# Three 256-column matmuls per weight tile in place of one of 512 and one of 256

## The reference

```
layer 0: x = LN(a*x + even_mixer(x));  x = LN(a*x + conv_ffn(x))     # HGRN2 scan, gated MLP
layer 1: x = LN(a*x + odd_mixer(x));   x = LN(a*x + conv_ffn(x))     # attention with rope
block 2: RG-LRU and dilated attention from one input projection, gates, output projections, RMS norm

conv_ffn(x):  h = x @ w_up                       # 2048 -> 2*5632
              h = conv over 3 tokens + bias
              return (silu(gate) * val) @ w_down # 5632 -> 2048
```

## Time and profile before

| | |
|---|---|
| time, median of 3 runs | 3618.95 us (3618.0 to 3619.64) |
| span of the profiled execution | 3619.8 us |
| TensorE matmuls | busy 3467.3 us, 96%, 19568 instructions |
| TensorE weight loads | busy 2989.3 us, 83%, 19568 instructions |
| VectorE | busy 2306.9 us, 64% |
| ScalarE | busy 1428.3 us, 39% |
| GpSimd | busy 405.6 us, 11% |
| HBM read | 594.43 MB, 165 GB/s over the span |

### The profile page before, as it was taken

How to read it: one execution, slowest core, us unless ns; L and a number is a source line. 1 busy time by engine, 2 the same in 40 slices (tenths; PEclk the granted TensorE clock), 3 DMA queues, 4 the chain that set the end, 5 groups by cost and what they waited for, 6 DMA issues and landing times.

```text
span 3619.8 us, 48876 instructions
## 1 busy us (share of the span) xinstructions
PE 3467.3 (96%) x19568; PEld 2989.3 (83%) x19568; DVE 2306.9 (64%) x2199; ACT 1428.3 (39%) x1113; POOL 405.6 (11%) x240
## 2 busy tenths in 40 slices
PE   8999899999999999899999999989999999999997
PEld 7888788888888888688888888878788788788886
DVE  5654667877764466467888764458666556545666
ACT  5542343333333345444333333345533333343332
POOL 1400130111111101030111111100000000000002
PEclk9999999999999999999999999999999999999999
DMA  5443245545555544144554555534454334435543
GB/s 209 175 176 143 75 151 183 181 181 185 185 182 187 186 145 163 59 163 167 182 184 185 182 183 189 186 129 153 163 181 177 140 140 174 151 133 185 183 178 134
DMA packets 84065, 598.16 MB, mean 165 GB/s; under 512 B 9329, under 2 KB 10481, under 8 KB 12146
## 3 DMA queue, kind: packets, MB, share of 16 engines
q1 hardware_dynamic: 81216, 589.34, 45.1%
q10 hardware_dynamic: 2738, 7.23, 0.6%
HBM read 594.43 MB, written 2.10 MB: 165 GB/s over the span
## 4 chain that ended last, share of the span: by engine, by line
PE 66%; issue 19%; DVE 7%; ACT 3%; POOLq 2%; POOL 1%; DVEq 1%; DMA 0%; ACTq 0%
PE acc L261 39%; PE acc L260 20%; DVE w_lo L192 4%; PE acc L257 3%; ACT w_hi L188 2%; POOLq L344 2%; PE acc L258 1%; PE acc L1429 1%; POOL over L342 1%; PE acc L1480 0%; DVE u_tiles L281 0%; PE acc L358 0%; PE acc L384 0%; DVE over L281 0%; POOLq L728 0%
## 5 line engine op out<-in xcount | busy, mean ns | idle before, releaser
L261 PE MATMUL acc<-x_hi_lo,w_hi 128*128 128x512 f32 x6720 | 2397.8, 398 | 0.0
L192 DVE TENSOR_TENSOR w_lo<-w_raw,w_hi 128x2048 fp32r<-128x2048 f32 x560 | 1382.4, 2469 | 1115.0 <-ACT w_hi L188 1113.8
L260 PE MATMUL acc<-x_hi_lo,w_lo 128*128 128x256 f32 x6720 | 1903.5, 283 | 14.5 <-DVE w_lo L192 14.5
L188 ACT ACTIVATE w_hi<-w_raw 128x2048 fp32r<-128x2048 f32 x560 | 1073.2, 1916 | 1977.7 <-PE acc L261 1977.7
L261 PEld LDWEIGHTS acc<-x_hi_lo,w_hi 128*128 128x128 f32 x6720 | 1267.7, 189 | 288.3 <-issue 4.1
L260 PEld LDWEIGHTS acc<-x_hi_lo,w_lo 128*128 128x128 f32 x6720 | 1276.0, 190 | 44.2 <-DVE w_lo L192 11.7
L261 PE MATMUL acc<-hidden_hi_lo,w_hi 128*128 128x512 f32 x1728 | 612.7, 398 | 0.0
L260 PE MATMUL acc<-hidden_hi_lo,w_lo 128*128 128x256 f32 x1728 | 485.6, 281 | 3.0 <-DVE w_lo L192 3.0
L261 PEld LDWEIGHTS acc<-hidden_hi_lo,w_hi 128*128 128x128 f32 x1728 | 324.6, 188 | 77.0
L260 PEld LDWEIGHTS acc<-hidden_hi_lo,w_lo 128*128 128x128 f32 x1728 | 326.5, 189 | 6.6 <-DVE w_lo L192 4.0
L257 PE MATMUL acc<-x_hi_lo,w_hi 128*128 128x512 f32 x448 | 181.0, 404 | 45.9 <-DVE w_lo L192 30.7
(11 more groups left out here) (250 smaller groups left out, 1687.0 us busy)
## 6 DMA issues: line engine op xcount, KB each, us to landing
w_raw<-weights_dram SPq DMA_DIRECT2D x560, 1024.0 KB, 4.8
resid<-x_dram ACTq DMA_DIRECT2D x4, 512.0 KB, 10.3
over<-w_gates_dram ACTq DMA_DIRECT2D x1, 2048.0 KB, 7.5
out_dram<-resid SPq DMA_DIRECT2D x4, 512.0 KB, 2.7
over<-con_dram ACTq DMA_DIRECT2D x5, 128.0 KB, 2.3
par<-par_dram ACTq DMA_DIRECT2D x1, 525.0 KB, 12.1
over<-con_dram ACTq DMA_DIRECT2D x2, 256.0 KB, 7.2
over<-gmlp_ws_dram ACTq DMA_DIRECT2D x1, 512.0 KB
```

The costliest lines, as they stand in the source:

```text
L188: nc.scalar.activation(whi[:, slot, :], raw[:, slot, :], ACT.Copy).then_inc(weights_hi, 1)
L192: nc.vector.tensor_tensor(wlo[:, slot, :], raw[:, slot, :], whi[:, slot, :].bitcast(F32), ALU.subtract).then_inc(weights_split, 1)
L260: nc.tensor.matmul(*rest, start=False, stop=False)
L261: last = nc.tensor.matmul(*both, start=False, stop=(k == CK * nch - 1))
```

## The change

Each weight tile gets three matmuls of 256 columns instead of one of 512 and one of 256. All three sum into the first 256 columns of the bank. w_hi is loaded twice per tile. The order is the same for all tiles: w_hi with the high part, w_lo with the high part, w_hi with the low part. Columns 256 to 511 of the banks are no longer written by these matmuls. The readout is a copy of 256 columns instead of a reduction over two halves of 256.

```diff
-                                both = (acc[:, bank, :], whi[:, s, w0:w0 + P], moving(k, 0, 2 * T))
-                                rest = (acc[:, bank, 0:T], wlo[:, s, w0:w0 + P], moving(k, 0, T))
-                                if k == 0:
-                                    nc.tensor.matmul(*both, start=True, stop=False)
-                                    last = nc.tensor.matmul(*rest, start=False, stop=False)
-                                else:
-                                    nc.tensor.matmul(*rest, start=False, stop=False)
-                                    last = nc.tensor.matmul(*both, start=False,
-                                                            stop=(k == CK * nch - 1))
+                                dst = acc[:, bank, 0:T]
+                                nc.tensor.matmul(dst, whi[:, s, w0:w0 + P], moving(k, 0, T),
+                                                 start=(k == 0), stop=False)
+                                nc.tensor.matmul(dst, wlo[:, s, w0:w0 + P], moving(k, 0, T),
+                                                 start=False, stop=False)
+                                last = nc.tensor.matmul(dst, whi[:, s, w0:w0 + P], moving(k, T, 2 * T),
+                                                        start=False, stop=(k == CK * nch - 1))
                         last.then_inc(chunk_used, 1)
...
-        def halves(bank):
-            return acc[:, bank, :].rearrange("p (h n) -> p n h", h=2)
-
         def read_out(dst, bank):
 
-            return nc.vector.tensor_reduce(dst, halves(bank), AX, ALU.add)
+            return nc.vector.tensor_copy(dst, acc[:, bank, 0:T])
```

## The result

The changed kernel takes 3686.82 us (median of 4 runs, 3686.25 to 3692.38) against 3619.3 us for the kernel before on the same chip: ratio 1.0189, 95% interval 1.0177 to 1.0201, +67.5 us. The forecast was 3609 us, a gain of 10; the time lies just inside the range given (3530 to 3690), on the other side.

A forecast was written before the change was run, and what follows sets the result against it. TensorE, busy 96% of the span, was taken as the bound, its 8960 matmul pairs of 352.1 ns making 87%. Forecast: 3619.0 + 0 for the matmuls - 9.9 for the readout = 3609 us, range 3530 to 3690.

The forecast's parts named there:

- f: Fixed time per matmul instruction beside its columns, in all 8960 weight tiles; taken as 0, so the stream changes by 0.
- rival 1: Each of 8960 tiles pays a fixed part for one more matmul with load: 3639 us, or 3672 at 7 ns; chance 0.25.
- plain fp32 rows: Matmuls stepping 216 ns at 256 columns and 111.6 at 128; gave the upper bound f = 7 ns, +63 us.
- 256 after 256: At a bank's first tile, L258 to L260 to L261 step 0.12 and 0.12 us: a load without slack costs nothing more.
- Instructions: TensorE gets six instructions per tile for four; sequencer not the bound, longer loop bodies fetched beside it: cost nothing.
- Readout: 512 readouts of 0.681 us become copies of 0.425; counted where they stand on the path, -9.9 us.
- the wait at L1452: In half0 and half1 the wait behind the readout falls from 2.6 to 1.6 us, -1.0 each.
- the 512-column form's own loss (2): The 10% loss belongs to 512-column matmuls or switching lengths: 3454 us at most, half of that 3531; chance 0.17.
- A shared path (3): Weight loads and moving data share a path in every tile: 396 ns per tile, 4003 us; chance 0.05.
- an unhidden load (4): The third weight load of each tile isn't hidden at all: 103 ns each, +923, 4532 us; chance 0.02.
- The overlap rule: Skill's rule that a load overlaps matmuls in flight only in another row group; would leave each tile's third load free-standing.

The follow-up runs named there:

- e5: Changed kernel with streams of one form per stage, varying moving columns, weight columns and matmuls per tile; steps of 114.9 ns at 248 moving columns to 226.8 at 512.
- e9: Kernel before with all 16 matmuls of one length in a chunk in a row, 512 first in even chunks, 256 first in odd; 3592.83 us, ratio 0.9918.
- e11: Kernel before with matmul order 512, 256, 256, 512, one change of length per tile instead of two; 3593.08 us in one run.
- e3: Changed kernel with fewer moving columns per matmul (240, 224, 192, 128, 64) in five stages, the rest of each product left out; 3934.61 us.
- e6: Changed kernel with other operand types in two stages, bf16 in up0 and plain fp32 in gates; 4142.55 us.
- e7: Changed kernel with both trips of down0 and down1 written out on TensorE instead of a loop over two; 3675.47 us, ratio 1.0150.
- e2: Kernel before with only the readout changed to a copy of columns 0 to 255, its own matmuls kept; 3610.49 us, ratio 0.9967.
- e1: Changed kernel with the third matmul summing into columns 256 to 511 and the old readout that adds the halves; 3696.72 us, ratio 1.0202.

## Why the prediction was wrong

The main step failed: "I take f = 0: 768 columns cost 352.1 ns either way". In the same stage they cost 352.7 ns before and 360.0 ns after, so f was 7.3 ns. The prediction named the right quantity and a rival of the right size (rival 1: f = 7, 3672 us), and chose the wrong end. Point by point:

- *Fixed part.* In a stream of one form it is 13.3 ns per matmul (e5), so three make 320 + 40 = 360 ns, as measured. Two would make 320 + 27 = 347, and e9 takes 347.5; the kernel before took 352 to 353, because its alternation wasted some 5 to 6 ns per pair (e9, e11). The difference of the two patterns, 13 - 6 = 7 ns, was the f to be used. I had split the pair's 352 ns by its own two steps, 118.7 and 234. Such a split can't separate a cost per matmul from one of the pattern: a cost that falls on the longer step looks like a slower rate per column. The sign was there: the 10% over 2.4 GHz of which I wrote that no row says where they go. In the mixed pattern the start times give 117 ns for a 256-column step and 236 for a 512-column one, where streams take 120 and 227: the split makes the short step 3 ns too cheap and the long one 9 too dear. The plain fp32 rows gave f = 7 by two lengths; I took them for the far bound. That they hit the size was luck: their 111.6 ns at 128 columns is the floor of 111.7 (e3), not columns plus a fixed part, and the fixed part of the 216 ns step is 2.7 (e6). Their 64 "matmuls" are also records of 32.
- *256 after 256.* The steps of 0.12 and 0.12 were read as "the usual step". At 10 ns the view can't tell 117 from 120, and 3 ns x 26,880 matmuls are 81 us. A finer reading would have misled as well: the start times give a median of 113 ns from L258 to L260 over the 512 places, and a stream takes 120. One such step between 512-column matmuls is no measure of a stream.
- *Price.* 560 chunks x 48 x 120 ns = 3225.6 us, against 3152.5 for the stream before (432 chunks of 5.653 and 128 of 5.550 us): +73.
- *Instructions.* "the longer loop bodies (...) are fetched beside it. Cost nothing" failed too. The sequencer's pace wasn't the bound, as said, but the way back in the loop of the down stages, whose body grew from 22 x 64 = 1408 to 22 x 96 = 2112 matmuls and loads, left TensorE without instructions for 4.7 and 4.1 us and at half clock behind. Written out, it goes: 14 us by the ratios (e7). The packets of q8 show the fetch: the body of 1408 is not fetched again for the second trip, that of 2112 is. At which length this turns, no run shows.
- *Readout.* -9.9 us forecast, -12 (-16 to -8) measured on the kernel before (e2), and about -5 by the ratios beside the three matmuls (e1). It holds on the kernel before, about half of it shows beside the three matmuls, and the wait at L1452 (now L1447) is 1.5 us where 1.6 was said.
- *Waits for w_lo.* Not foreseen: a chunk that takes 5.76 us covers more of a late split. Waits fall from 48.9 us to 41.2 with the old readout (e1), -8.

With the old readout that makes 73 + 14 - 8 = 79 us; e1 took 73 (67 to 79) more than the kernel before. The readout takes off another 5 to 10, which gives 69 to 74; measured 67.5. The terms come from different pairs of kernels, so they close to a few microseconds and no better.

Of the other rivals, the 512-column form's own loss (2) had a grain of truth, in the pattern. A shared path (3) would have made 396 ns, an unhidden load (4) over 450; both fall. The overlap rule that the prediction takes from the Trainium skill ("TensorE: Matmul & The Clock Gate"; it stands in the section "The mechanism") doesn't hold here: loads are busy for 150.00 of the 150.00 us in which matmuls are, all on the full array. The same page of the Trainium skill, section "LDWEIGHTS (loading the stationary operand)", gives P/1.2 ns for P columns, which is 107 ns for 128. At full clock the floor of 111.7 ns lies 5 ns above it; at half clock the floor is 213.3 (e3), twice the page's figure, so it goes with the granted clock.

## What to carry to other kernels

Price a matmul by a stream of its own form, at two lengths, and take columns at the clock plus a fixed part; don't divide the time of a mixed pattern among its members. With float32r at full clock, split a long matmul only if something pays 13 ns for each further one, and look at the instruction queue's packets when a loop body grows. Where operands become ready one after the other (the cast before the split), put the matmuls that need only the first in front: that and the order brought 2.2%.

## What the runs showed of the hardware

- The floor of a matmul with its load, float32r, all 128 rows and 128 weight columns: 111.7 ns at 2.4 GHz from 240 columns down to 128, 213.3 at 1.2 GHz with 128 and 64. Matmuls of 64 rows go below it: the 24 of the earlier trace rows, which take the two halves of the rows in turn, start two at a time, a few ns apart, every 111 to 112 ns.
- The fixed part shows at full clock alone. The kernel before and the changed kernel, both at granted clock 0.50 (TensorE's timeline, start us, duration us):

```profile
1305.14 0.63 PE L261 MATMUL acc<-x_hi_lo,w_hi 128*128 128x512 f32 x1
1305.57 0.41 PE L260 MATMUL acc<-x_hi_lo,w_lo 128*128 128x256 f32 x1
1305.78 0.63 PE L261 MATMUL acc<-x_hi_lo,w_hi 128*128 128x512 f32 x1
1306.21 0.41 PE L260 MATMUL acc<-x_hi_lo,w_lo 128*128 128x256 f32 x1
```
```profile
1185.92 0.41 PE L255 MATMUL acc<-hidden_hi_lo,w_hi 128*128 128x256 f32 x1
1186.14 0.41 PE L257 MATMUL acc<-hidden_hi_lo,w_lo 128*128 128x256 f32 x1
1186.35 0.41 PE L259 MATMUL acc<-hidden_hi_lo,w_hi 128*128 128x256 f32 x1
1186.57 0.41 PE L255 MATMUL acc<-hidden_hi_lo,w_hi 128*128 128x256 f32 x1
```

  Steps of 427 and 213 ns, and of 213 three times: 640 ns a tile either way, which is 768 columns at 1.2 GHz and nothing else. So neither the 13 ns nor the loss of the alternation is a number of TensorE's cycles, and at half clock the stream would have cost the same before and after.
- Streams of 128 or 64 columns ran for long at half clock. In down1 of e3 TensorE waited 1.2 us for a split at 2116 us, the granted clock fell from 1.00 to 0.50 at 2118 us and stayed there for 423 us, with TensorE recorded as busy for 417.72 of 420 us. In its gates stage the clock was 0.50 for 324 us, TensorE busy for 181.00 of 181 us within. So the kernel with less to multiply took 3934.61 us. In all the windows above with 192 columns or more it was 1.00.
- The fixed part depends on the type: 13.3 ns in float32r, 6.5 in bf16 read at a distance of 4 bytes, 2.7 in a record of fp32, two of which make a matmul, all at 256 columns. And on the weight tile: 9.3, 6.6 and 11.0 ns at 96, 64 and 32 weight columns. Why stays open.
- A loop body of 2112 matmuls and loads is fetched again for its second trip, one of 1408 is not; the longer one left TensorE standing for 4.7 and 4.1 us.
- Why strict alternation of 256 and 512 columns costs 5 ns a pair more than pairs of two stays open too.
